# A two-layer diffusion trunk step: where one tile's last expert choice, a tile's early start and the dot products stand in the order of work

## The reference

```python
sh1, sc1, g1, sh2, sc2, g2 = split(silu(cond) @ w_mod + b_mod, 6)
mix = token_mixing(modulate(x, sh1, sc1), p, lambda_init, cache)
x = layer_norm_affine(ALPHA * x + g1 * mix, ln1_g, ln1_b)
ffn = peer_ffn(modulate(x, sh2, sc2), w_q, subkeys, u, v)
x = layer_norm_affine(ALPHA * x + g2 * ffn, ln2_g, ln2_b)
```

## Time and profile before

| | us |
|---|---|
| median of 3 runs (3034.18 to 3035.61) | 3034.7 |
| profiled execution, its time | 3044.2 |
| profiled execution, its span | 3042.4 |
| busy: PE, DVE, POOL, ACT | 2174, 1727, 1466, 554 |
| DMA: moved, mean rate | 1071 MB, 352 GB/s |
| mean granted TensorE clock | 0.851 |

### The profile page before, as it was taken

The page is one execution under the profiler, slowest core; times in us unless marked ns, Lnnn a source line. Parts: engine busy times, 40 slices in busy tenths (PEclk is TensorE's granted clock), DMA queues, the critical chain, the costliest instruction groups (busy, mean ns, idle before and its releaser), DMA issues.

```text
span 3042.4 us, 29827 instructions
## 1 busy us (share of the span) xinstructions
PE 2174.3 (71%) x9748; PEld 1262.2 (41%) x9748; DVE 1726.7 (57%) x4339; ACT 553.7 (18%) x1609; POOL 1466.0 (48%) x1284
## 2 busy tenths in 40 slices
PE   7999949798952227455569559788988577776666
PEld 3786437674710013233345125566646232232223
DVE  1222998733079995444430764885122889866665
ACT  2221113321100111111111011232011232222221
POOL 0000545433368887676635664654452444444542
PEclk9999869899975568677779889789989898888898
DMA  9864979777899999999999989897996899999996
GB/s 393 327 214 165 365 288 337 283 294 287 307 408 409 387 366 388 410 409 409 409 387 365 409 306 368 305 326 284 362 337 230 360 421 418 414 392 422 422 421 278
DMA packets 259353, 1071.14 MB, mean 352 GB/s; under 512 B 29312, under 2 KB 32256, under 8 KB 225664
## 3 DMA queue, kind: packets, MB, share of 16 engines
q0 software_dynamic: 184320, 805.39, 67.6%
q1 hardware_dynamic: 71712, 253.28, 22.0%
q10 hardware_dynamic: 3168, 10.55, 0.9%
HBM read 1065.80 MB, written 3.31 MB: 351 GB/s over the span
## 4 chain that ended last, share of the span: by engine, by line
PE 39%; DMA 20%; DVE 18%; POOL 10%; issue 9%; another core or an unknown queue 2%; ACT 2%; SPq 0%; ACTq 0%; DVEq 0%; POOLq 0%
DMA ring<-in_peer_uv,experts 9%; PE psum L945 8%; PE psum L934 6%; PE psum L1104 5%; POOL ring L1861 5%; PE psum L852 5%; POOL work L1861 5%; DVE ring L1412 4%; PE psum L841 4%; PE psum L970 3%; DMA work<-in_peer_uv,experts 3%; DMA work<-in_peer_v,v_experts 2%; DMA ring<-in_peer_v,v_experts 2%; PE psum L1086 2%
## 5 line engine op out<-in xcount | busy, mean ns | idle before, releaser
L1861 POOL DMA_INDIRECT ring<-in_peer_u,experts x386 | 478.8, 1240 | 640.0 <-DVE experts L1661 312.3
L1861 POOL DMA_INDIRECT ring<-in_peer_v,v_experts x378 | 382.8, 1013 | 384.7 <-PE psum L841 247.9
L841 PE MATMUL psum<-ring,z 128*32 128x512 f32 x1512 | 257.6, 707 | 232.2 <-DMA ring<-in_peer_v,v_experts 152.2
L852 PE MATMUL psum<-work,wring 128*128 128x512 f32 x448 | 246.4, 699 | 155.3 <-ACT wring L1150 155.3
L945 PE MATMUL psum<-work,wring 128*128 128x256 f32 (+1 forms) x1744 | 327.6, 348 | 0.0
L1412 DVE CUSTOM_DVE_ANT_0 ring<-ring,h2a 128x1024 f32<-128x1024 f32 x256 | 304.3, 1219 | 19.3 <-DMA ring<-in_peer_u,experts 18.0
L945 PEld LDWEIGHTS psum<-work,wring 128*128 128x128 f32 x1744 | 287.7, 200 | 51.6 <-issue 19.9
L1861 POOL DMA_INDIRECT work<-in_peer_uv,experts x130 | 157.1, 1209 | 224.2 <-PE psum L852 173.6
L852 PE MATMUL psum<-ring,wring 128*128 128x512 f32 x392 | 205.3, 671 | 71.8 <-ACT wring L1150 71.8
L934 PE MATMUL psum<-wring,work 128*128 128x512 f32 (+1 forms) x548 | 220.4, 559 | 9.0 <-DMA wring<-in_wpack 4.5
L1861 POOL DMA_INDIRECT ring<-in_peer_uv,experts x126 | 150.0, 1191 | 146.5 <-PE psum L852 133.3
(11 more groups left out here) (205 smaller groups left out, 3189.4 us busy)
## 6 DMA issues: line engine op xcount, KB each, us to landing
wring<-in_wpack SPq DMA_DIRECT2D x380, 512.0 KB
ring<-in_wpack SPq DMA_DIRECT2D x88, 512.0 KB, 9.7
ring<-in_peer_u,experts POOLq DMA_INDIRECT x386
ring<-in_peer_v,v_experts POOLq DMA_INDIRECT x378
work<-in_rows ACTq DMA_DIRECT2D x4, 1024.0 KB
work<-in_peer_v,v_experts POOLq DMA_INDIRECT x134
work<-in_peer_uv,experts POOLq DMA_INDIRECT x130, 12.1
work<-in_rpb ACTq DMA_DIRECT2D x2, 1024.0 KB, 10.1
```

The source lines that it names most:

```text
L841: last = nc.tensor.matmul(psum[QUARTER * c:QUARTER * (c + 1), 6 + q, :], z[:, at:at + QUARTER], row(("v", n, o))[:, 512 * q:512 * (q + 1)] ...
L852: last = nc.tensor.matmul(psum[:, 6 + q, :], diag[:, SUM_NO[e] % SMALL, :], pair_of_rows(n, k)[:, D + 512 * q:D + 512 * (q + 1)], start=(k ...
L1861: pool.indirect_dma_start(dst, None, a["peer_" + what], bass.IndirectOffsetOnAxis(ap=index, axis=0)).then_inc(got[ROW_CELL[key]], 16)
```

## The change

Three things are moved and nothing of the computation changes. Tile 0's last group of the choice (and its index transpose) goes from ahead of the latents' norms to behind them, its pieces one by one behind the items `sgu` and `tt`, the rest ahead of `mq`. For that its scratch memory gets other addresses, the modulation's accumulator moves into z, z is cleared later, and the latents' cache load waits for the scores instead of the transpose.
Stage 3 gets an item `first` and its two `hT` in the third group of stage 2's choice, for its first tile alone; `begin` then does the second, and the first projection runs a tile at a time. Tile 3's eight dots ahead of tile 2's finish go back into their row.
The dots of tiles 0 and 3 are dealt by `free(x)`, which is the cost of items of `FREE_OF_VECTOR` and zero for others.

```diff
@@ stage_items
+    early = [("hT", m, 0, q) for q in range(2)] if m == LATENT[1] else []
-    out += [("hT", m, i, q) for i in range(T) for q in range(2)]
+    if not early:
+        out += [("hT", m, i, q) for i in range(T) for q in range(2)]
     for j in range(7):
-        out += [("proj", m, j, i) for i in range(T)]
+        for i in range(T):
+            if early and (j, i) == (0, 1):
+                out += [("hT", m, i, q) for q in range(2)]
+            out.append(("proj", m, j, i))
...
+                if m == CONTEXT[1] and (g, n) == (2, 0):
+                    out += [("first", LATENT[1])] + [("hT", LATENT[1], 0, q) for q in range(2)]
+def begun(kind, m):
+    if m == LATENT[1]:
+        return [0] if kind == "first" else [1]
+    return list(range(len(STAGES[m][1])))
@@ work
-    first = stages[0].index(("topk", 0, 0, 1, 0))
-    out, late = [], stages[0][first:]
+    first, last = stages[0].index(("topk", 0, 0, 1, 0)), stages[0].index(("topk", 0, 0, 3, 0))
+    out, late, behind_norms = [], stages[0][first:last], stages[0][last:]
...
         if x not in early:
+            if x == ("mq", 1, 0):
+                out += behind_norms
+                behind_norms = []
             out.append(x)
+            if x[0] in ("sgu", "tt"):
+                out += behind_norms[:1]
+                del behind_norms[:1]
@@
+FREE_OF_VECTOR = ("proj", "gate", "br", "pq", "mix", "topk", "mod")
+def free(x):
+    return cost(x) if x[0] in FREE_OF_VECTOR else 0
-def deal(first, last, steps):
+def deal(first, last, steps, cost=cost):
@@ schedule
-        first = PLACE[("topk", 0, 0, 1, 3)] if m == 0 else PLACE[("begin", 3)] + 1
+        first = PLACE[("topk", 0, 0, 1, 6)] if m == 0 else PLACE[("begin", 3)] + 1
-        lay(dots[8 * (m > 0):], first, late)
+        lay(dots, first, late, free)
-        set_(dots_of(3)[:8], done)
@@ tensor, proj
-                        if it[3]:
+                        j = it[2]
+                        apart = m == LATENT[1] and j == 0
+                        if it[3] and not apart:
                             continue
+                        mine = [it[3]] if apart else list(range(T))
...
-                            if q < 3:
+                            if q < 3 and mine[-1] == T - 1:
                                 last.then_inc(part_used, 1)
@@ scalar
-                        square_roots(T, 1.0)
+                        square_roots(len(begun(kind, m)), 1.0)
+                    elif kind == "first":
+                        square_roots(len(begun(kind, m)), 1.0)
-                            full(act, ("xi", m - 1, 0))
+                            full(act, ("xi", m - 1, 0) if l else ("ps", m - 1, 0, 3))
@@ vector
+                    if n == 0 and g == HEAD_GROUPS - 1:
+                        full(dve, modt(0, 11))
+                        nc.vector.memset(z[:, :], 0.0).then_inc(z_clear, 1)
-                nc.vector.memset(z[:, :], 0.0).then_inc(z_clear, 1)
-                    if kind == "begin":
+                    if kind in ("begin", "first"):
+                        mine = begun(kind, m)
                         if l:
-                            dve.wait_ge(x_ready, max(TILE_NO[(l - 1, t)] for t in tiles) + 1)
-                        for i in range(T):
-                            mean_var(i, x[:, tiles[i], :], D)
-                        roots(T)
+                            dve.wait_ge(x_ready, max(TILE_NO[(l - 1, tiles[i])] for i in mine) + 1)
+                        for k, i in enumerate(mine):
+                            mean_var(k, x[:, tiles[i], :], D)
+                        roots(len(mine))
```

More of the change, by code:

```diff
@@ L246, in work @@
                 del ahead[:1]
-    assert not ahead
+    assert not ahead and not behind_norms
     out += stages[2] + stages[3]
@@ L369, in schedule, with lay @@
     end = len(WORK)
-    def lay(items, first, last):
-        for x, place in zip(items, deal(first, last, items)):
+    def lay(items, first, last, cost=cost):
+        for x, place in zip(items, deal(first, last, items, cost)):
             at.setdefault(place, []).append(x)
@@ L472 @@
 for _x in WORK:
-    if _x[0] == "begin":
-        for _i in range(len(STAGES[_x[1]][1])):
+    if _x[0] in ("begin", "first"):
+        for _i in begun(*_x):
             _made += 1
@@ L499, in evacuator @@
     return FIXED_BY[kind]
-NO_PSUM = ("begin", "norms", "outs", "ln1_rows", "ln1", "topk", "u", "gm", "zf", "v", "fsum", "fin") + PAIR_WORK
+NO_PSUM = ("begin", "first", "norms", "outs", "ln1_rows", "ln1", "topk", "u", "gm", "zf", "v", "fsum", "fin") + PAIR_WORK
 ITEMS = [x for x in PROGRAM if x[0] not in NO_PSUM]
@@ L631, in __init__ @@
             self.cache = region(co, C_W)
-        mo = take(KD * N)
+        mo = self.merged_at = take(KD * N)
         self.merged = region(mo, KD * N).rearrange("p (k n) -> p k n", k=KD)
@@ L642, in __init__ @@
             assert 4 * N <= 3 * keys
-            self.nbs = region(take(768), 768).rearrange("p (r n) -> p r n", r=2)
+            self.nbs_at = take(768)
+            self.nbs = region(self.nbs_at, 768).rearrange("p (r n) -> p r n", r=2)
             self.turn = self.nbs.rearrange("p r n -> p (r n)")
@@ L654, in __init__ @@
         else:
-            self.modacc = region(take(1024) if base else KD * N, 1024).rearrange("p (c n) -> p c n", c=2)
+            self.modacc = None if base else region(KD * N, 1024).rearrange("p (c n) -> p c n", c=2)
             o = take(10 * P)
@@ L671, in __init__ @@
         small = cands + 2048
+        if base:
+            cands, small = CANDS_AT, SMALL_AT
         assert HG * 256 <= 1024 and (base or small + 896 <= MORE_AT)
@@ L685 @@
 HEAD_BASE = 10560
+CANDS_AT, SMALL_AT = 19296, 22368
 def build(nc, a, outs):
@@ L723, in build @@
         VIEW = [Views(work, M_WORDS, len(tiles), 0 if m else HEAD_BASE) for m, (_, tiles) in enumerate(STAGES)]
+        VIEW[0].modacc = z[:, 0:D].rearrange("p (c n) -> p c n", c=2)
+        assert VIEW[1].merged_at == CANDS_AT and VIEW[1].nbs_at == SMALL_AT
         def row(key):
@@ L921, in _ @@
                     elif kind == "proj":
-                        if it[3]:
+                        j = it[2]
+                        apart = m == LATENT[1] and j == 0
+                        if it[3] and not apart:
                             continue
-                        j = it[2]
+                        mine = [it[3]] if apart else list(range(T))
                         width = min(512, IN_W - 512 * j)
                         if j == 0:
-                            all_evacuated(pe, [("hT", m, i, q) for i in range(T) for q in range(2)])
-                        outb = [room(("proj", m, j, i)) for i in range(T)]
+                            all_evacuated(pe, [("hT", m, i, q) for i in mine for q in range(2)])
+                        outb = {i: room(("proj", m, j, i)) for i in mine}
                         for q in range(4):
                             w = slot(("in", m, j, q), 2)
-                            for i in range(T):
+                            for i in mine:
                                 for k in range(2):
@@ L1684, in _ @@
                     T, N = v.T, v.N
-                    if kind == "begin":
+                    if kind in ("begin", "first"):
+                        mine = begun(kind, m)
                         if l:
-                            dve.wait_ge(x_ready, max(TILE_NO[(l - 1, t)] for t in tiles) + 1)
-                        for i in range(T):
-                            mean_var(i, x[:, tiles[i], :], D)
-                        roots(T)
-                        for i in range(T):
-                            normalised(m, i, i)
+                            dve.wait_ge(x_ready, max(TILE_NO[(l - 1, tiles[i])] for i in mine) + 1)
+                        for k, i in enumerate(mine):
+                            mean_var(k, x[:, tiles[i], :], D)
+                        roots(len(mine))
+                        for k, i in enumerate(mine):
+                            normalised(m, i, k)
                     elif kind == "modt" and EVAC_BY[INDEX[it]] == "v":
```

## The result

The changed kernel takes 3051.7 us (median; 3046.4 to 3053.4), the kernel before 3034.7 (3034.2 to 3035.6) beside it: ratio 1.0056, interval 1.0045 to 1.0066. It is slower by 17 us; the forecast was 11 us faster, and the range ended at 3049.

The account below looks back on a forecast made before the run. Four stretches outside the DMA-saturated row gathers were taken to decide the time, rows and weights at DMA rate setting the norms. Terms -15 - 1 + 11 + 8 + 8 make 11 us less than 3034.7, 3024; range 3002 to 3049.

Parts of the forecast that it names:

- Stretch 1: 312 to 412 us, tile 0's last choice group behind the norms: norms 3 us later, first score 475, 15 us lost.
- Stretch 2: 460 to 630 us, the latents' heads, dots only behind projections, gates and products: 11 us won (0 to 17).
- I leave half of their waits, some 4 us won: Other four differential heads of stage 1: each gate covers two or three dots, halving waits for softmax weights, some 4 us.
- the 6 us of the first four heads: First four differential heads of stage 1, without a gate beside them: 5 or 6 dots leave the softmax weights' way, 6 us.
- heads don't give: Rival: waits on line 1783 move to the products' passes, 16 of 19 us gone, 3040; chance 0.14.
- Stretch 3: 1771 to 1948 us, second latent mixing tile by tile: projections 17 us earlier, norms 3 later, 8 us won (-12 to 26).
- Stretch 4: 1948 to 2095 us, the second mixing's heads, reckoned as the first mixing's: 8 us won (0 to 12).
- The dots pace the gathers: Rival: a gather costs 2.29 us throughout, norms 7 us later in stage 1, 20 in stage 3; 3051, chance 0.14.
- The decision point: Gathers' issue ahead of the norms: from about 2.0 us a row on, it would decide the time.
- Rows keep pace: Rival: rows ahead of both norms keep up, norms at 407 and 1877, 8 + 18 us more won, 2998; chance 0.14.
- Early start void: Rival: tile 1's early start in stage 3 gives nothing, path through tile 2 and rows; 8 us gone, 3032; chance 0.08.
- The root: Row-gather stretches 836 to 1140 and from 2366 change length by no more than 3 us, else prediction wrong at root.

Follow-up runs that it names:

- capped: Changed kernel with at most 39 of tile 0's and 44 of tile 3's dots ahead of the norms, the rest dealt freely behind; 3033.1 us, ratio 0.9992.
- heads_free: Changed kernel without the moved group, old dealing up to the first score of stages 1 and 3, free dealing from there; 3035.5 us, ratio 1.0005.
- narrow_weights: Changed kernel, the 20 weight loads of projections 1 to 5 of stage 3 loading only half their columns; one execution 3037.9 us.
- part 2: Of the change, stage 3's early first tile, first projection a tile at a time, eight dots ahead of the finish gone; alone 3026.8 us.
- only_early: Changed kernel with the moved group and the free dealing undone, so only stage 3's early tile is left; 3026.8 us, ratio 0.9969.
- half dots: Changed kernel, each dot of tile 3 summing 512 columns instead of 1024, rows still coming whole; one execution 3039.0 us.
- after_again: The changed kernel once more, unchanged, for a second profile; median 3051.5 us, ratio 1.0066, profiled execution 3046.6 us.
- first_20: Changed kernel with only the early tile and old dealing, but 20 of tile 0's dots ahead of stage 1's norms; 3015.6 us, ratio 0.9937.
- only_free: Changed kernel with only the free dealing kept, 65 and 68 dots ahead of the norms of stages 1 and 3; 3054.7 us, ratio 1.0062.

## Why the prediction was wrong, point by point

**Stretch 1: right in kind, 9 us short.** The step that failed is the sum of bytes, 40.5 MB at 405 GB/s. The rate was right (401 in 315 to 425). But 29.0 MB of rows had come by then, not 27.3, since the ring loads three rows ahead of the dot that is due; 13.6 MB of weights, not 13.2; and 1.9 MB of ScalarE's own loads (the latents' cache and a bias table, issued at 408.5). I had seen that the cache load now starts ahead of the norms and costed it at nothing. Together 44.5 MB, 4.0 more, which is 10 us at 405; the norms began at 424.8 for my 415 (1.7 us of this is the profile's own shift). The 3 us that I added for the first row's way stand on no row, and were not needed: 44.5 MB at 405 GB/s are the 110 us that passed. This is the trace's account; a run that takes bytes away was made for stage 3 alone. The rest held: norms to gating product 18.3 us (18.4 predicted), from there to the first score 42.5 (41.5). A side effect that I had not seen: ScalarE's gelu of dots 0 to 31 now stands ahead of the copy that TensorE needs (ScalarE waits 16.8 us for the dots), so the first gate of stage 1 comes 11 us late. In `capped` it is on time.

**Stretch 2: the step "I leave half of their waits, some 4 us won" failed, and the 6 us of the first four heads with it.** 0.5 us instead of 11. The part up to score 12 gave more than I took (6.1 us, at a clock of 1.00 for 0.88), scores 16 to 20 gave 4.8 in the change, at a clock of 0.83 for 0.72, but only 0.6 in `heads_free` at 0.72. Then score 22 to xw takes 41.2 us instead of 28.3. I had looked at how the gate covers its dots, not at where the last of the 128 come: they are what gm and xw wait for. In the change one more head stands ahead of xw, too, since `late`, a share of the way from `first`, moved on with `first` and the moved group. The rival "heads don't give" named the outcome in this mixing and not the mechanism: it had the waits on line 1783 move to the products' passes, but TensorE's wait on the softmax weights stayed, 20.3 us where the earlier trace rows had 15.8, and VectorE's wait for the products went from 4.1 only to 6.2.

**Stretch 3: projections nearly right, rows 8 us short.** Tile 1's second half began at 1802.8 (1794 and a shift of 12.8 make 1806.8), finish and normalisation were done 15.2 us behind the last v step (18.7 predicted), the gates ended 14.4 us nearer (17; against the first profile of before, on which the 17 was worked out, it is 18.8). The norms began at 1915.4, 133.7 behind that v step (1781.7) for my 126.1. The step that failed is again the sum of bytes. From the point where I counted, 1801.6 with the shift, 30.1 MB of rows and 15.2 of weights came, 45.3 MB for my 41.5: 3.8 MB, 9 us. Again the rate was right, the amount not: I counted half of the ten slots behind the projections, and no rows in flight. That these bytes decide is what `narrow_weights` shows. So part 2's gain, which `only_early` shows, was eaten here by 27 more dots ahead of the norms than its 39.

**Stretch 4: 5.5 for 8.** From score 0 to 16 the change gives 6.2 us (85.4 for 91.6), at a clock of 1.00 for the 0.93 of the earlier trace rows; behind it nothing more.

**The sum.** The four stretches came out 9, 10.5, 10.6 and 2.5 us worse than forecast, the v steps 2.6 better, and the 1 us for the clearing of z shows nowhere: 29 us, which makes 18 slower, in these two profiles, of 11 faster. Some 16 of the 29 are the bytes ahead of the two norms (8 and 8), 10.5 the first heads. Against the first profile of before, stretch 3 gains 2.1 us instead of losing 2.6, the v steps gain 8.3 instead of 2.6 and the heads of stage 1 gain 3.0 instead of 0.5; so a single pair of profiles does not give these parts to better than 2 to 6 us. The waits for the two norms and the score behind the first come out alike in both pairs.

**The rivals.** "The dots pace the gathers" gave 3051, the measured time, for a reason that doesn't hold. The issue is shorter with half dots, 955 ns for 1129, and the norms at 152.6 and 152.3 us say that it decides nothing here. I had also read the earlier trace rows wrongly: VectorE wasn't at rest at 1787.74, it was in the finish of tile 2 (1785.3 to 1799.0), so the 0.94 us hold beside that work too, and the 1.99 beside dots. The Trainium skill (SBUF — State Buffer, "SBUF: two separate sides") says that GpSimd can't write descriptors while VectorE runs an instruction in a 2-port performance mode, and that an instruction with two inputs in SBUF, as a dot is, holds the shared port only against GpSimd instructions that read SBUF. So it doesn't say that dots hold up the writing of descriptors, as I had taken it; which part of an issue they lengthen, no run here shows. The decision point I gave, 2.0 us a row, was not reached: 65 gathers in 127 us, with 47.7 us of idling for cells among them, are 1.95 each. "Rows keep pace" failed on the bytes. "Early start void" is refuted by `only_early`. The 358 GB/s that the Trainium skill (DMA: Bandwidth & Descriptors, "Specifications") gives are passed by the 407 to 410 here, as in the trace of before.

**The root** held: tile 0's v steps 19 to 31 take 257.9 us before and 258.7 after, the tail 703.9 and 703.9.

**Left open.** How much of stage 1's gain up to score 12 is the clock and how much is order wasn't separated. `capped` gives back 20 us behind the first score of stage 3, 12 of them up to score 16, where VectorE is 83.8 of 97.3 us busy for 70.3 of 85.4 and the clock is 0.91 for 1.00; which of the two it is wasn't tried. Why one profile of before lost 15 us in untouched row stretches wasn't tried.

## What to carry to other kernels

A rule that puts small work "only where the engine is free" also decides how much of it stands ahead of each wait: count it at every barrier first (here worth up to 18 us, the placing among the heads 3), with the time of a barrier as the later of two: VectorE's own work ahead of it, and all bytes that the queues bring until then, run-ahead and other queues included, over the rate. Deal work that must end by a point so that its last pieces aren't bunched in front of what waits for them. And work that moves off one wait leaves idle time behind and may fill a stretch where its engine has none: look at both.

## What had not been expected of the hardware

The DMA engines moved 407 to 408 GB/s for 100 us (1812 to 1912) in 4 KB rows beside weights, at shares of 1.02 and 1.03. Two profiled executions of one kernel differed by 16 us, and executions of the kernel before ran from 3026 to 3045, so that a pair of profiles can hide a difference of 17; here it could be followed only in the second pair, item by item. The granted clock of one stretch of 245 matmuls, score 0 to 12 of stage 1, was 1.00, 0.94, 0.87 or 0.86 in `after_again`, `heads_free`, `only_early` and `first_20`, with 49.8, 52.9, 55.9 and 59.1 us (1.00 is the 2.4 GHz level, a mean below it a mixture with 1.2). The matmuls are the same, the dots beside them are not (21, 23, 26 and 33). The first of them:

```profile
482.70:532.50 49.80, 47.39 (x245) 38.47 (x245) 37.76 (x89) 20.84 (x55) 23.58 (x20) 1.00 0.73 269
```

TensorE had waited 36.5 us for the norms ahead of it where it was 1.00, and some 20 in the other three; of these `heads_free`, with the dots out of the way, had the 0.94. But `only_free` had 1.00 as well (49.6 us), with 21.9 us of that wait; ahead of it TensorE had waited 27.8 us for the choice's indices (14 to 16 in the others, 2 in `first_20`). So what the free dealing gained in the change may be clock as well as order, and which wait gives the clock isn't shown.
